# A two-block sequence model on one Trainium2 core: moving a maximum to ScalarE's sums, and the last gates' product behind the first scores

## The reference

```python
# first attention (differential): 8 heads, two score sets each
q, k, v, g = split(rms(x) @ w_in)            # w_in: 1024 x 4096
a = softmax(q1 @ k1.T) - lam * softmax(q2 @ k2.T)   # causal
o = rms(a @ v) * (1 - lambda_init)
x = x + (o * silu(g)) @ w_out
# second attention (stick breaking): 16 heads
z = q @ k.T / 8                              # causal, strictly below the diagonal
a = exp(log_sigmoid(z) + cumsum_from_the_right(log_sigmoid(-z)))
x = x + ((a @ v) * silu(g)) @ w_out
```

## Time and profile before

| | |
|---|---|
| Median of 3 runs | 2466.69 us (2463.56 to 2467.03) |
| The profiled execution's own time | 2455.28 us |
| Its span, first to last instruction | 2453.5 us |
| Busy over the span | PE 96%, DVE 61%, ACT 40%, POOL 9% |
| First attention's loop, 1386.7 to 1606.0 (219.3 us) | PE 175.8, DVE 180.0, ACT 181.5 us busy; TensorE clock 0.93 |
| Second attention's loop, 2047.4 to 2345.0 (297.6 us) | PE 271.8, DVE 275.6, ACT 232.3 us busy; clock 0.98 |

### The profile page before, as it was taken

The page is one execution under the profiler, slowest core; times in us unless marked ns, Lnnn a source line. Parts: engine busy times, 40 slices in busy tenths (PEclk is TensorE's granted clock), DMA queues, the critical chain, the costliest instruction groups (busy, mean ns, idle before and its releaser), DMA issues.

```text
span 2453.5 us, 30299 instructions
## 1 busy us (share of the span) xinstructions
PE 2347.8 (96%) x12882; PEld 1252.3 (51%) x12882; DVE 1500.1 (61%) x1888; ACT 983.5 (40%) x1478; POOL 213.5 (9%) x258
## 2 busy tenths in 40 slices
PE   7999999999999999999999877899999999989999
PEld 5445444444444444444544455654444446777764
DVE  6898755644644455587632288865534405998961
ACT  5245344221212122433331378852323215777841
POOL 0001030000000000624301101012000000000000
PEclk9999999999999999999999899999999999999999
DMA  4011010202110101103011000021131100000021
GB/s 182 35 69 35 1 35 35 103 35 69 40 64 35 69 35 69 37 1 138 35 69 65 5 1 1 1 104 35 69 137 35 70 1 1 1 36 1 1 86 52
DMA packets 50344, 116.02 MB, mean 47 GB/s; under 512 B 2403, under 2 KB 7836, under 8 KB 49825
## 3 DMA queue, kind: packets, MB, share of 16 engines
q1 hardware_dynamic: 48472, 105.40, 12.1%
q10 hardware_dynamic: 1736, 8.68, 0.9%
HBM read 101.49 MB, written 12.58 MB: 46 GB/s over the span
## 4 chain that ended last, share of the span: by engine, by line
PE 78%; DVE 14%; ACT 6%; issue 1%; DMA 1%; ACTq 0%; POOL 0%; DVEq 0%
PE PS L72 74%; PE PS L75 3%; DVE RG L107 3%; ACT RG L81 3%; DVE R L93 2%; DVE mx L110 2%; DVE R L101 2%; DVE RG L93 2%; DVE RG L101 1%; ACT OV L84 1%; DVE scl L110 1%; DMA RG<-in_a_w_in 1%; ACT R L81 1%; DVE oss L110 1%; ACT mx L81 0%
## 5 line engine op out<-in xcount | busy, mean ns | idle before, releaser
L72 PE MATMUL PS<-R,RG 128*128 128x512 f16 (+1 forms) x5472 | 1165.8, 375 | 6.9 <-DVE R L93 2.8
L72 PEld LDWEIGHTS PS<-R,RG 128*128 128x128 f16 (+1 forms) x5472 | 541.8, 103 | 627.3 <-issue 13.3
L72 PE MATMUL PS<-RG,R 128*128 128x512 f16 x2880 | 630.6, 379 | 3.3 <-DVE R L101 2.8
L72 PEld LDWEIGHTS PS<-RG,R 128*128 128x128 f16 x2880 | 281.3, 98 | 334.5 <-DVE R L101 3.2
L81 ACT ACTIVATE R<-PS,scl 128x512 f32<-128x512 f32 (+1 forms) x192 | 126.7, 686 | 712.5 <-PE PS L72 611.7
L101 DVE SCALAR_TENSOR_TENSOR R<-PS,scl,R 128x512 f32<-128x512 f32 (+1 forms) x208 | 148.5, 746 | 143.5 <-PE PS L72 121.2
L101 DVE SCALAR_TENSOR_TENSOR RG<-RG,scl 128x4096 f16<-128x4096 f32 (+2 forms) x52 | 190.5, 3664 | 53.7 <-ACT RG L81 53.7
L107 DVE TENSOR_TENSOR_SCAN RG<-RG 128x127 f32<-128x127 f32 (+7 forms) x128 | 168.3, 1342 | 86.5 <-ACT RG L81 86.5
L72 PE MATMUL PS<-R,OV 128*128 128x64 f32 (+2 forms) x1456 | 198.2, 278 | 7.5 <-DVE R L93 5.2
L110 DVE TENSOR_REDUCE scl<-RG 128x1 f32<-128x4096 f32 (+2 forms) x39 | 155.0, 3975 | 65.8 <-DMA RG<-in_a_w_in 26.2
L81 ACT ACTIVATE RG<-RG,scl 128x4096 f16<-128x4096 f32 (+2 forms) x52 | 158.6, 3050 | 89.7 <-DVE scl L113 89.7
(11 more groups left out here) (126 smaller groups left out, 1550.0 us busy)
## 6 DMA issues: line engine op xcount, KB each, us to landing
RG<-in_w_ff SPq DMA_DIRECT2D x16, 2048.0 KB, 8.2
RG<-in_a_w_in SPq DMA_DIRECT2D x8, 2048.0 KB, 8.6
xspill<-R ACTq DMA_DIRECT2D x2, 4096.0 KB, 15.7
RG<-in_w_kv SPq DMA_DIRECT2D x4, 2048.0 KB, 8.1
RG<-in_b_w_in SPq DMA_DIRECT2D x4, 2048.0 KB, 8.0
RG<-in_w_in SPq DMA_DIRECT2D x3, 2048.0 KB, 8.2
R<-in_x SPq DMA_DIRECT2D x8, 512.0 KB, 8.0
RG<-in_w_out SPq DMA_DIRECT2D x2, 2048.0 KB, 7.8
```

The lines of the kernel that those rows point to most:

```text
L72: return self.engine.matmul(*a, **k) if self.engine else Nothing()
```

## The change

There are two parts.

1. In the second attention the eight maxima of the gated tiles leave VectorE. ScalarE takes in their place the sum of absolute values of each row (`gate_sum`: one ACTIVATE Abs of 128x1024 with its accumulator), which is an upper bound of the maximum. It stands in ScalarE's loop at u = the tile's last group + 4, behind the copy of group u-1 and ahead of the sigmoids of group u+1.
2. In the first attention the gates' product of tile 7 moves: the order on TensorE is scores 0, scores 1, product 28 of tile 7, scores 2, product 29 of tile 7, scores 3. As weights 28 and 29 are then still in use, the buffers of groups 0 to 3 (EA) and 0 to 2 (E2) move to RG[0:3584], where raw weights lie. So the load of raw weight 31 waits until those groups have been transposed, and its four maxima move from u = 8 to 11 to u = 16 to 19. Products of tiles 6 and 7 get banks 6 and 7. On ScalarE, Silu of tile 7 stands behind the exponentials of group 2, and a one-element Exp stands ahead of the loop and behind that Silu; the copy of transposed group 0 moves behind them. The maxima of gates' tiles 6 and 7 on VectorE move to u = 4 and u = 5.

```diff
+        def ea(u):
+            return RG[:, 512 * u:512 * u + 512] if u < 4 else EA[u % 4]
+        def e2(u):
+            return RG[:, 2048 + 512 * u:2560 + 512 * u] if u < 3 else E2[u % 3]
...
-            for t in range(NT):
+            for t in range(NT - 1):
                 if t == 2:
                     bound(30)
                 for c in range(2):
-                    product_n(28 + c, t, ("gg", t, c))
+                    product_n(28 + c, t, ("gg", t, c), bank=6 + c if t == NT - 2 else None)
...
-            for u in range(N + 3):
-                if u < N:
+            scores(0)
+            scores(1)
+            product_n(28, NT - 1, ("gg", NT - 1, 0), bank=6)
+            scores(2)
+            product_n(29, NT - 1, ("gg", NT - 1, 1), bank=7)
+            for u in range(2, N + 3):
+                if u == 2:
+                    scores(3)
+                if 4 <= u < N:
                     scores(u)
                 turn_a(u - 2, 0)
...
# vector
-                if t < NT - 1:
+                if t < NT - 2:
                     gate_peak(t)
...
-                if u == 3:
+                if u == 4:
+                    gate_peak(NT - 2)
+                if u == 5:
                     gate_peak(NT - 1)
                     e.wait_ge(*step.last())
                     e.tensor_reduce(col(123), col(32, 8), AX.X, ALU.max).then_inc(*sig("o_peak").up())
-                if 8 <= u < 12:
-                    j = u - 8
+                if 16 <= u < 20:
+                    j = u - 16
...
-                if u >= 3 and sb_groups[u - 3][1][-1] == 15:
-                    i = sb_groups[u - 3][0]
-                    e.wait_ge(*sig("g_gated").at(i, 1))
-                    e.tensor_reduce(col(24 + i), GG[:, i, :], AX.X, ALU.max,
-                                    apply_absolute_value=True).then_inc(*sig("g_peak").up(i))
# scalar
+            for t in range(NT - 1):
+                if t == 3:
+                    convert(30)
+                gate_silu(t)
+            e.activation(lamt[:, 7:8], epst[:, 0:1], ACT.Exp).then_inc(*sig("table").up())
...
+                if u == 0:
+                    e.wait_ge(*sig("weight").at(30))
...
-                turned(u - 1, 0)
+                if u == 2:
+                    gate_silu(NT - 1)
+                    e.wait_ge(*sig("table").at())
+                    e.activation(lamt[:, 7:8], epst[:, 0:1], ACT.Exp)
+                    turned(0, 0)
+                if u >= 2:
+                    turned(u - 1, 0)
...
+            def gate_sum(i):
+                e.wait_ge(*sig("g_gated").at(i, 1))
+                e.activation(dg[:, :, :].rearrange("p t q -> p (t q)").bitcast(F16), GG[:, i, :], ACT.Abs,
+                             accum_out=col(24 + i)).then_inc(*sig("g_peak").up(i))
...
-            for u in range(N + 2):
+            for u in range(N + 4):
...
                 turned(u - 1, 0)
+                if u >= 4 and sb_groups[u - 4][1][-1] == 15:
+                    gate_sum(sb_groups[u - 4][0])
# sync
+                if i == 31:
+                    e.wait_ge(*sig("bank_full").at("ta", 3, 0))
+                    e.wait_ge(*sig("joined_a").at(2))
```

More of the change, by code:

```diff
@@ L488, in product_t, with product_n @@
                 last_product[i] = key
-            def product_n(i, t, key, ready=None):
-                b = banks.take(key)
+            def product_n(i, t, key, ready=None, bank=None):
+                b = banks.take(key) if bank is None else banks.take_at(key, bank)
                 e.wait_ge(*sig("weight").at(i))
@@ L848, in turn_a @@
                     for x in range(0, n, 128):
-                        mm = e.transpose(b[:, x:x + 128], EA[v % 4][:, at + x:at + x + 128], ident[:, :])
+                        mm = e.transpose(b[:, x:x + 128], ea(v)[:, at + x:at + x + 128], ident[:, :])
                     mm.then_inc(*full.up("ta", v, s))
             N = len(da_groups)
-            for u in range(N + 3):
-                if u < N:
+            scores(0)
[7 more added lines that the diff above has]
+                if 4 <= u < N:
                     scores(u)
@@ L1679, in vector @@
                     w, n = width(i), len(hs)
-                    a, a2 = EA[v % 4], E2[v % 3]
+                    a, a2 = ea(v), e2(v)
                     ri, ro = oss[:, 8 * (v % 2):8 * (v % 2) + n], oss[:, 8 * (v % 2) + 4:8 * (v % 2) + 4 + n]
@@ L1712, in vector @@
                                     apply_absolute_value=True).then_inc(*step.up())
-                if u == 12:
+                if u == 20:
                     e.wait_ge(*step.last())
@@ L2228, in scalar, with gate_silu @@
                         *banks.empty([("vv", c, t)], sig("bank_act"), "vv", c, t))
-            for t in range(NT):
-                if t == 3:
-                    convert(30)
+            def gate_silu(t):
                 for c in range(2):
@@ L2265, in exp @@
                 w = width(i)
-                out = EA[u % 4] if c == 0 else E2[u % 3]
+                out = ea(u) if c == 0 else e2(u)
                 e.wait_ge(*sig("top_a").at(u, c) if u >= da_first else sig("top_a").at(u, 1))
```

## The result

| | Median, us | Runs | From to |
|---|---|---|---|
| Kernel before, timed beside the changed one | 2465.12 | 4 | 2460.48 to 2467.03 |
| Changed kernel | 2440.72 | 4 | 2436.45 to 2447.21 |
| Kernel before, in all later draws together | 2455.7 | 91 | 2450.37 to 2468.99 |
| Changed kernel, this draw and two later ones | 2440.6 | 16 | 2435.37 to 2447.21 |

A forecast was written before the change was run, and what follows sets the result against it. Bounds: ScalarE's pace as the first loop's pipeline fills, VectorE at the changed places of the second. First loop 6.3 us plus second 6.0 make 12.3, off the median 2466.69: 2454.4 us, range 2449.5 to 2463.5.

The forecast's parts named there:

- The base: Whole kernel: the predicted gain of 12.3 us was subtracted from the median 2466.69 us, not from the profiled 2455.28.
- About 0.8 of 1.13 is won. Seven times 0.8 is 5.6.: Second loop: each maximum removed from VectorE brings a later scan about 0.8 us forward; 5.6 us, bounds 0 and 7.9.
- The 0.4 of the tail: Behind the second loop: tile 7's Abs runs beside the factor's small instructions; 0.4 us won, bounds 0 and 1.1.
- The start: Start of the first loop: scores begin earlier and group 3's scaling comes at 1395.6 instead of 1402.77, 7.2 us earlier.
- The switches of tables: ScalarE, start of first loop: each table switch takes 1.28 us; with a drain, two added switches leave some 2.8 less.
- VectorE's maxima and the quarters: First loop: moved gate maxima gain 1.2, lose 1.2 and 0.6 us; weight 31's four maxima give 3.9, take 4.2.
- The clock stayed at 1.00 under both products: Rival, first loop: TensorE's clock halves under the moved products; both 2467.4 us, one about 2460; chance 0.10.
- VectorE was the bound at the places of the second part: Rival, second loop: VectorE isn't the bound, only the first loop's 6.3 us is left, 2460.4; one-part cases together 0.18.
- the first lead was kept: Rival, first loop: added work is paid in full later, so only the second part counts, 2460.7; one-part cases together 0.18.
- no table load came with Abs: Rival, second loop: each Abs brings two table loads, 2.6 us, making the kernel slower, 2474.8 us; chance of slower 0.06.
- The second loop, from 297.6 to 292: Second loop: sign expected in the trace after, the loop's length falling from 297.6 to 292 us.

The follow-up runs named there:

- fillers at the ends and at the start: Kernel before plus 16 idle matmuls ahead of TensorE's second-attention waits: only at the seven tile ends 2452.06 us, only for the first four groups 2460.22 us.
- the sums alone: Kernel before with only the second attention's maxima replaced by ScalarE's Abs sums, first attention as before: 2448.70 us, ratio 0.9961.
- the tiny sums: Kernel before with the second attention's maxima replaced by ScalarE sums over only 8 of each row's 1024 values: 2443.72 us, ratio 0.9942.
- the later sums: Changed kernel with each Abs sum one group later on ScalarE, the last tile's where it was: 2436.72 us, 0.9916 of the kernel before.
- order alone: Kernel before with only the first attention's new order, the second attention's maxima left on VectorE: 2452.38 us, ratio 0.9978.
- the quarters at 8 to 11 in the changed kernel: Changed kernel with the four maxima of raw weight 31 moved back to u = 8 to 11: 2446.28 us, 0.9951 of the kernel before.

## Why the prediction was wrong

Both parts of the change work as said, and the number missed the range. What failed, in order of size:

1. **The base.** "I take the difference from the sum and subtract it from the median": the median of three runs, 2466.69. 17 of the 91 later runs lie above 2463.5 and the median is 2455.7, so this base was 11 us too high. My own profiled execution, 2455.28, stood almost on that median; by it the sum gives 2443.0, 2.3 from what was measured. I had noted the 11.4 us between the two and asked nothing of it. Why the first draw was high isn't shown: the clock of those three runs isn't on record. By the 91 later runs, three in a row above 2463.5 would be rare, so that the chip or the hour had a part is a rival that no run here tests. The range had to hold both bases.
2. **A term that the sum lacked.** Waits of TensorE were priced by their length only. But the wait behind a maximum is also where half-clock stretches begin (shown by the fillers at the ends and at the start). Removing the maxima ends or shortens six of these seven waits: the sums alone gave 9.5 us, the tiles at full clock about 4.5, and the clock, higher by 0.0027 over the runs, about 4.1. The split is an estimate. In single traces it can't be seen, since the stretches come and go; in tiles 4 and 5 of the changed kernel's three traces they came each time.
3. **"About 0.8 of 1.13 is won. Seven times 0.8 is 5.6."** Mis-sized: 0.3 and 0.37 in tiles 6 and 7, 0.61 in 5, 0.72 in 2, 1.13 in 3. I let ScalarE "make up the rest within a few groups"; for a pair of groups of one head it doesn't, since both sigmoids stand behind the Abs (shown by the tiny sums and by the later sums, which win the rest), and so does the copy that TensorE awaits. That this term was too large and the one above was missing partly cancel: that the second loop comes out 5.4 us shorter in the mean of four traces each, near my 5.6, is in part luck. The 0.4 of the tail can't be told: from the last scan to the span's end it is 112.8 to 114.5 us in the traces with maxima and 112.1 to 113.8 in those with full sums where they were.

By the other steps:

- *The start.* Predicted 7.2 us earlier, measured 7.65 (7.25 in a later trace of the changed kernel, against the same trace of before). No idle ahead of the scores, blocks of 5.34 us (5.2 said), Silu 0.06 us behind the second.
- *The switches of tables.* 1.28 us, with the next ACTIVATE starting 0.01 us behind the load's end (1386.81 + 1.28, Silu at 1388.10). The Trainium skill ("ScalarE: Activation LUTs", section "What ACT_TABLE_LOAD costs") adds a drain of about 1.38 us; this trace shows none here, and the measurement decides.
- *VectorE's maxima and the quarters.* The lead over the kernel before, by the scalings, is 7.65 us at group 3, 6.95 at group 8, 10.94 at 12, 11.85 at 16, 7.83 at 21 and 7.3 at the end. The maxima took 0.7 here, but 0.2 in five of the eight other traces of this order and 0.7 to 1.1 in three: I had said 0.6. The quarters gave 4.0 back (groups 9 to 12) and took 4.0 (17 to 20), 3.9 and 4.2 said. The 0.9 between groups 12 and 16 isn't theirs: it also comes with the quarters left at 8 to 11, and in the second trace of the kernel before.
- *The rivals.* The clock stayed at 1.00 under both products. VectorE was the bound at the places of the second part, until ScalarE took over in part; the first lead was kept (order alone: 0.9978); no table load came with Abs. Of the Trainium skill's rule on short idles between groups of matmuls ("TensorE: Matmul & The Clock Gate", section "A second HAM failure mode: psum-queue depth-cycling") I had made a rival for the first loop. There its condition wasn't met, as no idle was left under the products. In the second loop the trace agrees with it: 1.30 us idle, then clock 0.50.
- *The second loop, from 297.6 to 292.* The two profiled executions show nothing of it (293.3 and 293.7 us from first to last scan); the one after had 10.2 us more at half clock. Read tile by tile, and over four traces of each kind, it is there.

**Open.** Why the kernel before took over 2460 us in all four runs of the first draw. How often the stretches come in each kernel, and why a wait of about the same length starts one in one execution and none in another. Why the filler at the start alone, and the quarters at 8 to 11 in the changed kernel, gave slower runs at a lower mean clock.

## What to carry to other kernels

Before a difference is subtracted from a median, compare that median with the profiled execution and with the spread of the runs: a gap between them is itself a finding, here 11 us, nearly as much as the whole gain that I forecast. In a loop that three engines hand around, read each repeated piece by itself and compare only pieces at full clock; price a wait of TensorE at its length plus the half-clock stretch that may follow it. And when work moves to an engine with room, ask what stands right behind it there, and who waits for that: one place later in ScalarE's order took away TensorE's waits of 1.0 to 1.6 us and was worth 2 us in the traces (4 by the medians, 2440.6 to 2436.7). Look also at what a filler itself must await: it helps only if it can start before the wait does.

## What the runs showed of the hardware

- In a loop of otherwise dense work the granted clock fell from 1.00 to 0.50 in some executions and some places, mostly at a wait of TensorE of 1.0 to 2.5 us or shortly behind one (1.30 us in tile 6 of the kernel before); in tile 4 three falls came behind waits of 0.6 us. A tile hit by it was 1.5 to 4.4 us longer (4.4 in tile 7 with the filler at the start, 60.64 us against 56.24). Over 91 runs of one kernel (2450.37 to 2468.99 us, mean clock 0.992 to 0.981) the time rose by about 1.5 us for each 0.001 of clock lost.
- Sixteen matmuls that compute nothing, about 1 us, put ahead of these waits, made the kernel before faster by 0.22% (0.9978, 0.9966 to 0.9991). The same ones made the changed kernel slower by 0.24% (0.9955 against 0.9931): there they came behind a wait for a bank (1.04 us), which they didn't shorten.
- An ACTIVATE Abs of 128x1024 from SBUF with its accumulator is two instructions, 1.06 and 0.19 us; the next ACTIVATE started 1.05 us behind the first one's start (2289.00 to 2290.05). With VectorE's maxima left in place, eight of them cost nothing that could be measured (0.9997, 0.9982 to 1.0012).
